# State-space features of a third head pair made beside the shifted projections of a two-block transformer kernel

## The reference, cut to what matters

```python
def gmlp_spatial_gating(pu, pv, ln_g, ln_b, w_s, b_s):
    u = gelu(pu)
    v = layer_norm_2(gelu(pv), ln_g, ln_b)          # "spatial norm"
    s = einsum('gts,bnsgd->bntgd', w_s * tril, vc) + b_s
    return u * s

def rwkv7_time_mix(p, mu, ...):
    p = p + (token_shift(p) - p) * mu               # every unit is "shifted"
    r, k, v, wd, ad, gd = split(p)
    wlog = -softplus(-(w0 + tanh(wd) @ w_up)) - 0.5
    decay = exp(-exp(wlog))
    a = sigmoid(a0 + ad @ a_up)
    g = sigmoid(gd) @ g_up
    kk = heads(k * k_k);  kk = kk / norm(kk)
    k = k * (1 + (a - 1) * k_a)
    y = scan(step, 0, (r, decay, k, v, -kk, kk * a))
    return ((norm(y) * lnx_g + lnx_b) + sum(r * k * r_k) * v) * g
```

## Time and profile before

| | |
|---|---|
| median of 3 runs | 1571.79 us (1570.42 to 1573.23) |
| the profiled execution's own time | 1572.88 us |
| its span | 1570.8 us |
| head (first unit to the first matmul of round 1) | 934 to 1031.6 us |
| round 1 | 1031.6 to 1085.6 us |

### The profile page before, as it was taken

One profiled execution on the slowest core, in us unless ns is written; L12 is line 12 of the kernel. 1 busy time (PEld: TensorE's weight loads), 2 busy tenths in 40 slices (PEclk: granted clock), 3 DMA queues, 4 the chain that ended last, 5 costly groups with the idle time before them and its releaser, 6 DMA issues.

```text
span 1570.8 us, 25892 instructions
## 1 busy us (share of the span) xinstructions
PE 1518.1 (97%) x10408; PEld 1252.6 (80%) x10408; DVE 1093.5 (70%) x1898; ACT 749.5 (48%) x1253; POOL 191.9 (12%) x159
## 2 busy tenths in 40 slices
PE   7999999999999999999999999988898999999998
PEld 6878786888888877777788888767767899989886
DVE  5999994666655478758544747886547978867556
ACT  5544455535522477747632625654424544444223
POOL 2435364500010000000004000000000000000000
PEclk9999999999999999999999999999999999999999
DMA  6323243454465323232424232210002233433331
GB/s 220 94 86 120 90 147 108 160 165 146 147 184 182 116 86 95 90 111 81 147 95 142 74 121 81 81 43 4 3 29 86 90 108 106 123 97 121 101 98 54
DMA packets 45798, 166.18 MB, mean 106 GB/s; under 512 B 5280, under 2 KB 5408, under 8 KB 45680
## 3 DMA queue, kind: packets, MB, share of 16 engines
q1 hardware_dynamic: 43056, 155.95, 30.8%
q0 software_dynamic: 2624, 8.59, 1.9%
HBM read 162.42 MB, written 2.10 MB: 105 GB/s over the span
## 4 chain that ended last, share of the span: by engine, by line
PE 79%; DVE 15%; ACT 3%; issue 2%; DMA 0%; SPq 0%; DVEq 0%; ACTq 0%
PE bank L643 24%; PE bank L645 24%; PE bank L644 23%; DVE bank L2390 7%; PE bank L1366 1%; PE bank L1218 1%; ACT scratch L654 1%; DVE small L2416 1%; DVE x_rows L2390 1%; PE bank L1197 1%; DVE scratch L2387 0%; DVE weight_lo L699 0%; PE bank L1463 0%; ACT weight_hi L691 0%; DMA x_in<-in_x 0%
## 5 line engine op out<-in xcount | busy, mean ns | idle before, releaser
L691 ACT ACTIVATE weight_hi<-raw 128x1024 fp32r<-128x1024 f32 x195 | 205.8, 1057 | 384.6 <-PE bank L645 381.1
L643 PE MATMUL bank<-h_T_hi,weight_hi 128*128 128x512 f32 (+1 forms) x848 | 342.0, 403 | 2.8 <-DVE conv_in L2387 2.1
L699 DVE TENSOR_TENSOR weight_lo<-raw,weight_hi 128x1024 fp32r<-128x1024 f32 x138 | 168.8, 1224 | 238.6 <-ACT weight_hi L691 238.6
L645 PE MATMUL bank<-h_T_hi,weight_lo 128*128 128x512 f32 (+1 forms) x848 | 329.8, 389 | 0.0
L644 PE MATMUL bank<-h_T_lo,weight_hi 128*128 128x512 f32 (+1 forms) x848 | 329.2, 388 | 0.0
L643 PEld LDWEIGHTS bank<-h_T_hi,weight_hi 128*128 128x128 f32 x848 | 160.1, 189 | 43.2 <-issue 8.5
L2390 DVE SCALAR_TENSOR_TENSOR bank<-conv_in,columns,bank 128x512 f32<-128x512 f32 x240 | 181.4, 756 | 8.3
L644 PEld LDWEIGHTS bank<-h_T_lo,weight_hi 128*128 128x128 f32 x848 | 160.3, 189 | 33.5 <-issue 3.6
L645 PEld LDWEIGHTS bank<-h_T_hi,weight_lo 128*128 128x128 f32 x848 | 159.8, 188 | 33.8
L699 POOL TENSOR_TENSOR weight_lo<-raw,weight_hi 128x1024 fp32r<-128x1024 f32 x57 | 141.8, 2488 | 154.1 <-ACT weight_hi L691 154.1
L643 PE MATMUL bank<-h_T_hi,half_weight_hi 128*128 128x256 f32 (+1 forms) x240 | 79.1, 330 | 0.0
(11 more groups left out here) (500 smaller groups left out, 3193.0 us busy)
## 6 DMA issues: line engine op xcount, KB each, us to landing
raw<-in_weights SPq DMA_DIRECT2D x289, 512.0 KB, 3.5
x_in<-in_x SPq DMA_DIRECT2D x4, 512.0 KB, 5.8
x_rows<-in_x POOLq DMA_DIRECT2D x4, 512.0 KB, 4.9
out<-x_rows SPq DMA_DIRECT2D x3, 512.0 KB, 2.6
mem_in<-in_mem POOLq DMA_DIRECT2D x2, 512.0 KB, 4.2
ln_rows<-in_ln_g POOLq DMA_DIRECT2D x4, 256.0 KB, 4.4
ln_rows<-in_ln_b POOLq DMA_DIRECT2D x4, 256.0 KB, 5.1
silu_row<-in_c POOLq DMA_DIRECT2D x1, 512.0 KB, 6.6
```

Source lines behind the costliest of these rows:

```text
L643: pe.matmul(o, lhs[0], rhs[0], start=start, stop=False, skip_group_check=onto)
L645: return pe.matmul(o, lhs[1], rhs[0], start=False, stop=stop, skip_group_check=onto)
L691: act.activation(weight_parts(u)[0][:, :], raw[u % RAW][:, :], ACT.Copy).then_inc(*weight_hi.up(u))
L699: engine.tensor_tensor(lo[:, :], raw[u % RAW][:, :], view(hi[:, :]), ALU.subtract).then_inc(*ready.up(u))
```

## The change

It makes the features of pair 2 in the head too, between tokens(0) and tokens(1); starts the chain at place 4; reorders the units so that each is there for its step; moves tanh to place 1 and the sigmoid of units 13 and 14 to place 7; drops PE's own table; gives the spatial mix two banks (4 and 5) and the features and tokens of the head the other two (6 and 7); puts `sg_out` before the spatial norm in DVE's loop body; and gives the spatial norm's tiles, the bias rows and `Bw` of pair 2 places of their own. For room, GpSimd's area for DMA descriptors is set to 8192 bytes. Round 1 is then chunks(0), chunks(1), features(3).

```diff
-SHIFT_ORDER = (12, 13, 14, 0, 4, 1, 5, 8, 9, 2, 6, 10, 3, 7, 11)
+SHIFT_ORDER = (12, 4, 0, 13, 14, 8, 5, 1, 9, 6, 2, 10, 7, 3, 11)
-HEAD_STEPS = {6: 1, 7: 3, 8: 2, 9: 2, 10: 2, 11: 2, 12: 2, 13: 2, 14: 2}
-PE_HEAD_STEPS = HEAD_STEPS | {10: 0, 11: 4}
+HEAD_STEPS = {4: 1, 5: 2, 6: 2, 7: 3, 8: 2, 9: 2, 10: 2, 11: 3, 12: 2, 13: 3, 14: 3}
-    Bw = [second(f"Bw{n}", [P, S]) for n in range(2)]
+    Bw = [second(f"Bw{n}", [P, S]) for n in range(3)]
     here = Map(nc, loose_at, END)
-    u_T = here("u_T", [P, FW, S])
-    v_sg = here.pair("v_sg", [P, MIX])
+    here.at = END // 64 * 64 - 34 * 1024
...
+    v_tiles = [here(f"v_tile{n}", [P, S]) for n in range(TT)]
+    u_T = here("u_T", [P, FW, S])
-    feature_places = bank_ring((4, 5, 6, 7))
+    mixed_places, feature_places = bank_ring((4, 5)), bank_ring((6, 7))
-    sg_ring = place_ring((0, 1, 2, 3))
+    sg_ring = place_ring((), v_tiles)
-    s_out_ring, product_ring = place_ring((), (scratch[7], scratch[6])), place_ring((), scratch[5:8])
+    s_out_ring, product_ring = place_ring((), (scratch[7], scratch[4])), place_ring((), scratch[5:8])
@@ pe_second_in
-                bank = side.take(pe, ("sg", t), sg_out, t)
+                bank = mixed_places.take(pe, ("sg", t), sg_out, t)
-            head_steps(head, i, PE_HEAD_STEPS)
+            head_steps(head, i)
     def feature_banks(f):
+        return feature_places if f < 3 else wide
+
+    def token_banks(f):
         return feature_places if f < 2 else wide
@@ pe_features
         if f == 0:
-            pe.wait_ge(*lora_ready.at("gd"))
+            pe.wait_ge(*lora_ready.at("tanh"))
@@ pe_states
+        if f == 0:
+            pe.wait_ge(*lora_ready.at("gd"))
     def head_features(features, tokens):
-        return itertools.chain(features(0), features(1), tokens(0), tokens(1))
+        return itertools.chain(features(0), features(1), tokens(0), features(2), tokens(1))
@@ rwkv_rounds
-        interleave(chunks(0), chunks(1), itertools.chain(features(2), features(3)))
+        interleave(chunks(0), chunks(1), features(3))
@@ act_second_in
+            if i == 1:
+                act.wait_ge(*shift_done.at(12))
+                activate(act, lora_in[0:HALF, :], lora_in[0:HALF, :], ACT.Tanh).then_inc(*lora_ready.up("tanh"))
             if i == 4:
                 act_identity(act)
+            if i == 7:
                 act.wait_ge(*shift_done.at(14))
-                activate(act, lora_in[0:HALF, :], lora_in[0:HALF, :], ACT.Tanh).then_inc(*lora_ready.up("tanh"))
                 activate(act, gd_T[:, :, :], gd_T[:, :, :], ACT.Sigmoid).then_inc(*lora_ready.up("gd"))
@@ dve_second_in: these five lines, unchanged but for the bank, now stand ahead of dve_spatial(dve, i)
             if 3 <= i < 3 + TT:
                 t = i - 3
                 s = s_out_ring.take(dve, t, ya_lo, t)
                 dve.wait_ge(*sg_mixed.at(t))
+                dve.tensor_tensor(s, mixed_places["sg", t], rows[2][:, :], ALU.add).then_inc(*sg_out.up(t))
...
+            if i < TT:
+                dve_spatial(dve, i)
@@ dve_features
-        if f == 0:
-            dve.wait_ge(*ya_lo.at(TT - 1))
-        if f > 1:
+        if f == 3:
             dve.wait_ge(*pe_c.at(f - 2, "LM", 1, 1))
-        mult(dve, Bw[f % 2][:, :], f_kk[f][:, :], f_wall[:, :]).then_inc(*dve_f.up(f, "Bw"))
+        mult(dve, weighted(f)[:, :], f_kk[f][:, :], f_wall[:, :]).then_inc(*dve_f.up(f, "Bw"))
-    nc = bacc.Bacc("TRN2", target_bir_lowering=False, num_devices=1)
+    nc = bacc.Bacc("TRN2", target_bir_lowering=False, num_devices=1, dynamic_dma_scratch_size=8192)
```

More of the change, by code:

```diff
@@ L404, in build @@
     Bw_at = second.at
-    Bw = [second(f"Bw{n}", [P, S]) for n in range(2)]
+    Bw = [second(f"Bw{n}", [P, S]) for n in range(3)]
     loose_at = second.at
     here = Map(nc, loose_at, END)
-    u_T = here("u_T", [P, FW, S])
-    v_sg = here.pair("v_sg", [P, MIX])
+    here.at = END // 64 * 64 - 34 * 1024
     w_s = here("w_s", [P, 4 * P])
     w_sp = here.pair("w_sp", [P, 4 * P])
+    v_sg = here.pair("v_sg", [P, MIX])
     rows = [here(f"rows{n}", [P, S]) for n in range(4)]
+    v_tiles = [here(f"v_tile{n}", [P, S]) for n in range(TT)]
+    u_T = here("u_T", [P, FW, S])
     here = Map(nc, Bw_at, loose_at)
@@ L424, in build @@
     here, there = Map(nc, B_AT, M_AT), Map(nc, loose_at, END)
+    f_sq, f_a, f_kk = ([scratch[n], None, scratch[n], None] for n in (2, 1, 6))
+    f_sq[1], f_a[1], f_kk[1] = (there(f"f_{c}1", [P, S]) for c in ("sq", "a", "kk"))
     work, tokens = [], []
@@ L430, in build @@
         tokens.append([(here if n else there)(f"tok{n}{c}", [P, TT, P]) for c in "kv"])
-    state_at = there.at
     chunk_state = [(here(f"P_T{n}", [P, NC, CHUNK]), here(f"Z{n}", [P, NC, CHUNK])) for n in range(2)]
-    there = Map(nc, state_at, END)
-    f_sq, f_a, f_kk = ([scratch[n], None, scratch[n], None] for n in (2, 1, 6))
-    f_sq[1], f_a[1], f_kk[1] = (there(f"f_{c}1", [P, S]) for c in ("sq", "a", "kk"))
     f_sq[3], f_a[3], f_kk[3] = scratch[7], here("f_a3", [P, S]), here("f_kk3", [P, S])
@@ L1321, in pe_second_in, with weighted @@
                 done.then_inc(*sg_mixed.up(t))
-            head_steps(head, i, PE_HEAD_STEPS)
+            head_steps(head, i)
     def feature_banks(f):
+        return feature_places if f < 3 else wide
+    def token_banks(f):
         return feature_places if f < 2 else wide
+    def weighted(f):
+        return Bw[2 if f == 2 else f % 2]
     def pe_features(pe, f):
@@ L1352, in pe_tokens @@
         for n, (source, step) in enumerate(((AR[:, f, 0, :], "A"), (f_kk[f][:, :], "be"), (f_a[f][:, :], "ke"), (v_T[:, f, :], None))):
-            bank = feature_banks(f).take(pe, ("tok", f, n), act_f, f, "tok", n)
+            bank = token_banks(f).take(pe, ("tok", f, n), act_f, f, "tok", n)
             if step:
@@ L1415, in matrices @@
                         heads, tok = head_rows(j), slice(n * P + part * CHUNK, n * P + (part + 1) * CHUNK)
-                        lhs = Bw[f % 2][heads, tok] if source == 0 else k_T[heads, f, tok]
+                        lhs = weighted(f)[heads, tok] if source == 0 else k_T[heads, f, tok]
                         done = pe.matmul(pair[j][cut(part, CHUNK), cut(n)], lhs, AR[heads, f, :, tok], start=True, stop=True)
@@ L2202, in act_tokens @@
                 act.wait_ge(*pe_c.at(f - 2, "ZY", 1))
-            bank = feature_banks(f)["tok", f, n]
+            bank = token_banks(f)["tok", f, n]
             if n == 0:
@@ L2883, in dve_second_in @@
             fused(dve, o[:, 1:S], p[:, 0:S - 1], column("mu_shift_2", n), o[:, 1:S], ALU.mult, ALU.add).then_inc(*shift_done.up(n))
-            if i < TT:
-                dve_spatial(dve, i)
             if 3 <= i < 3 + TT:
@@ L2889, in dve_second_in @@
                 dve.wait_ge(*sg_mixed.at(t))
-                dve.tensor_tensor(s, side["sg", t], rows[2][:, :], ALU.add).then_inc(*sg_out.up(t))
+                dve.tensor_tensor(s, mixed_places["sg", t], rows[2][:, :], ALU.add).then_inc(*sg_out.up(t))
                 dve.wait_ge(*sg_out.at(t))
                 mult(dve, grid(s), grid(s), u_T[:, :, cut(t)]).then_inc(*sg_out.up(t, "gated"))
+            if i < TT:
+                dve_spatial(dve, i)
             if 4 <= i < 4 + TT:
```

## The result

The changed kernel takes 1594.96 us (median of 5 runs, 1592.5 to 1597.1) against 1570.94 for the kernel before (5 runs): 1.0146 of its time, 95% interval 1.0134 to 1.0158, or 24 us slower. The forecast was 1588.4, slower, with a range that holds the result; two of its terms turned out wrong. The profiled execution after has a time of 1596.87 and a span of 1594.8.

The account below looks back on a forecast made before the run. PE, busy 97% of the span, bounds the kernel. A place-by-place walk of three engines gave head 20.0 us later, less 0.1 idle, round 1 6.2 shorter, clock 2.9: +16.6 us, 1588.4 us, range 1578 to 1598.

Parts of the forecast that it names:

- The banks of the mix: Head: with two banks, PE waits 2.9 us before the third spatial mix and 0.4 before the fourth for DVE's reads.
- The wait for pair 1's squares: Head, before `kk` of pair 1: PE waits 8.4 us for ACT's `sq`, which ends at 1004.4.
- the 0.8 of pair 0: Head, place 4: PE wants the first `sq` at 976.6, ACT has it at 977.4, a wait of 0.8 us.
- The transposes: Head, two banks copied by a late ACT: PE waits 1.6 us at place 11 and 4.0 at place 14.
- Moved work: Pair 2's `w`, `a` and `kk`, 1.9 us of PE, go from round 1 to the head; sum nil.
- loads: SP's loads have a place more in the new order: no cost.
- removed waits: Waits dropped (`y_a` before `f_kk`, pair 2's `Bw`) ended nothing on PE's path: no gain.
- The descriptor area: Smaller area for POOL's loads: taken as 0 us, bounds 0 and 3, since loads are issued a stage ahead.
- the faster rival: Head hides the third pair, costing only 1.9 us, if `sq` and banks are there by 996: 1567.5; 8%.
- Round 1: Without pair 2's chain, waits at levels 2 to 5 shrink: 47.8 of 54.1 us, 1.9 moved, 4.3 gained.
- Clock: Half rate after the head waits of 8.4 and 4.0 us: 2.9 us lost for both, bounds 0 and 7.
- The slower rival: Each of three long waits brings a clock drop, the last reaching into round 1: 24 us slower, 1596; 15%.

Follow-up runs that it names:

- Experiment 11: Changed kernel with start at unit 6, both old step tables, third pair in round 1, and banks 4 to 7 all shared by mix and features: 1575.24 us, 1.0023.
- experiment 6: Kernel before, with only the third pair's features moved into the head (start at unit 6, third weighted tile, smaller descriptor area, more steps from place 11): 1590.83 us, 1.0109.
- 9: Changed kernel with level products of two neighbouring blocks as one 64-row by 128-column matmul, leaving out every second block's own weights: 1585.41 us, 1.0090.
- 12: Changed kernel with the third pair back in round 1 and level products of two neighbouring blocks as one matmul: 1583.37 us, 1.0082.
- 5: Changed kernel with start at unit 6, both step tables of before and the third pair in round 1, split banks kept: 1582.61 us, 1.0062.
- 1: Changed kernel with the third pair's features put back into round 1, start at unit 4 kept: 1590.17 us, 1.0120.
- 3: Changed kernel with four banks (4 to 7) instead of two for the token parts of pairs 0 and 1: 1595.55 us, 1.0155.
- experiment 4: Changed kernel with seven matmuls of no use ahead of TensorE's 7.0 us wait for pair 1's squares: 1596.83 us, 1.0155.
- 8: Changed kernel with both four banks for the token parts and seven matmuls of no use ahead of the wait for pair 1's squares: 1594.83 us, 1.0137.
- experiment 2: Changed kernel with TensorE's own step table, skipping place 8 and doing four steps at place 9: 1595.27 us, 1.0150.
- experiment 7: Changed kernel with 64x64 level, identity-started and values' products replaced by half as many 128-row by 64-column matmuls with identity weights: 1648.53 us, 1.0478.
- experiment 10: Kernel before with the third pair's features alone in the head, plus seven and five matmuls of no use in its two long waits: 1592.82 us, 1.0136.

## Why the prediction was right, and where it was wrong

Right, by its steps:
- *The banks of the mix* (2.9 and 0.4 forecast): 2.64 and 0, ended by DVE's bias add at 965.83. Experiment 11 shows the split of the banks as the cause.
- *The wait for pair 1's squares* (8.4): 7.00. ScalarE's squares ended at about 1004.0, not 1004.4, and TensorE stood there at 997.1, not 996.0, behind a half-rate stretch from 966.7. The same delay probably covered the 0.8 of pair 0, for which TensorE did not wait.
- *The transposes* (1.6 and 4.0): 1.5 (1.30 and 0.20) and 4.00.
- Moved work, loads, removed waits: nothing that the traces show. The descriptor area no run changes alone; order, tanh, places and the area cost 3.6 us together (experiment 11).
- *The verdict*: the faster rival needed ScalarE's squares by 996; they came 8 us later. The pair's own work in the head also costs more than it brings (experiment 6, 17 us).

Wrong:
- *"Round 1: ... The walk makes 47.8 of 54.1 us: 1.9 moved, 4.3 gained."* It is 53.7. The walk let the waits for DVE and ScalarE shrink and had no term for TensorE's own instructions; one such wait went, and "issue" waits came in its place. This was the step that the text named as the one a round of 54 us would make wrong. Experiments 9 and 12 show a gain of the forecast size (47.8 against 52.8 with the clock out) once a third of round 1's matmuls is gone.
- *"Clock: ... I take 2.9"*, mis-sized: the first matmul came at 1057.53, where the walk without clock, moved by the earlier start of 1.1, has 1050.4. That is 7.1 us net, the end of the bounds of 0 and 7. It hides two larger errors that partly cancel, which is luck. TensorE's busy time in the head grew by 12.2 us (109.5 against 97.3); 1.9 of it is moved work, so 10.3 go with the lower clock. Its idle time grew by 14.8 us, where the walk has 18.0 (waits of 18.1, less the 0.1): 10.3 - 3.2 = 7.1. The waits of 2.6 and 1.3 us were each followed by 6.8 us at half rate, the one of 4.0 by 3.4; at the one of 7.0 (997.1 to 1004.1) 6.8 us began at 1000.8, inside the wait, so about half of it cost nothing:

```profile
965.00:973.50 8.50, 7.67 (x25) 5.28 (x26) 6.75 (x12) 3.95 (x9) 0.00 (x0) 0.60 0.20 62
999.50:1007.50 8.00, 3.37 (x6) 2.10 (x7) 5.82 (x8) 7.88 (x10) 0.00 (x0) 0.58 0.03 4
1027.00:1035.00 8.00, 7.80 (x20) 4.82 (x19) 3.41 (x5) 4.36 (x6) 0.00 (x0) 0.57 0.19 66
```

So the forecast's 16.6 lacks 4.2 of the clock and 5.9 of round 1, and leaves out the 1.1 and 1.8 by which the start and round 2 came out shorter; with 0.2 behind the rounds, 16.6 + 4.2 + 5.9 - 1.1 - 1.8 + 0.2 = 24.0. The slower rival (1596) has the measured +24 us by luck: the clock was dear, as it says, but it still counts round 1's 6.2 us, and that missing gain weighed more than what its clock term has over the forecast's.

What the parts of the change cost, by the ratios one upon another: order, tanh, places and descriptor area 3.6 us (experiment 11), the split banks 6 (5), the start at unit 4 without TensorE's own table 9 (1), the pair in the head 4 (the change, in intervals that touch). Put in alone, the pair costs 17. That the early start had already paid for part of its waits would explain the difference, but is not shown.

**Still open:** what holds the "issue" waits. A block of instructions is transferred 1 to 2 us behind each, and fewer matmuls end them, but whether it is the transfer or TensorE's queue itself no run here separates. Nor did a run show why some waits bring the half rate and others do not.

## What to carry to other kernels

A round with many small matmuls can be held by TensorE's instructions while the page shows the engine idle: before moving another engine's work out of it, look for "issue" waits and for instruction blocks that already come one upon another, and test the gain with fewer matmuls before counting on it. In a stretch in which TensorE never waits, the engines that feed it can have idle time on average but little in order: once TensorE waits for ScalarE, each new instruction of ScalarE ahead of the awaited one can cost its full length. Giving each user its own banks halves the ring of both; it cost 6 us here, more than order, tanh, places and descriptor area together (3.6).

## What the hardware showed that was not expected

- A half-rate stretch does not follow from the wait before it alone. The wait of 2.6 us for the third mix was followed by one in the changed kernel and in experiments 1, 3, 4, 8, 9 and 12, but not in 2, 5 and 7. The wait of 1.3 us at the transposes was followed by one in the changed kernel and not in experiment 4, where it is as long. In experiment 2 the windows behind its wait of 2.6 us and behind the one of 2.7 us at 1005 read 1.00; the rate falls only at 1021, at the wait of 6.0 us:

```profile
965.00:976.00 11.00, 8.40 (x41) 6.14 (x40) 9.03 (x13) 5.27 (x11) 0.00 (x0) 1.00 0.21 54
1004.00:1014.00 10.00, 8.73 (x37) 6.91 (x38) 8.40 (x11) 7.97 (x11) 0.00 (x0) 1.00 0.19 54
1021.00:1033.00 12.00, 7.98 (x23) 5.25 (x24) 7.39 (x10) 7.59 (x11) 0.00 (x0) 0.57 0.24 82
```

- Half-rate time taken away at one place came back in part at others (experiments 4, 8), and the time did not follow it: the granted clock of the whole span is 0.988 in the changed kernel, 0.990 and 0.992 in these two, at nearly the same time. In experiment 10 a head without any was no faster at all.
- A 128-row float32 matmul of 64 columns takes 0.11 us in a row (experiment 7). One of 64 rows by 128 columns takes 0.03 (64 of them in 1.98 us), and in a level 64 rows by 64 columns take 0.015 (117 of them from 1090.76 to 1092.51 after the change). Two 64-column matmuls in one of 128 columns left TensorE's busy time in round 1 nearly where it was (43.45 against 44.20 us) with a third fewer instructions.
